# Moving the SBUF addresses of the operands of TensorE in an encoder trunk with experts

## The chip, the cores and the metric

One core of one Trainium2 chip. The metric is the device time of one execution in microseconds (us), less is better. Before the change it is 2148.49 us, the median of three runs (2148.49 to 2149.2).

## What is computed

A trunk of two layers over 256 tokens of width 1024, in float32. Each layer takes a root-mean-square norm, projects it to 59 tiles of columns for four token mixers (dilated attention, a conformer convolution, a state-space scan, a Fourier mix), gates and adds their outputs, and projects them back. Then comes a feed-forward part: dense SwiGLU (2816 wide) in layer 0, and in layer 1 a mixture of 8 experts, each SwiGLU 3584 wide, of which each token takes two. A gated per-layer embedding closes each layer.

```python
for l in range(DEPTH):
    xn = rmsnorm(h, norm_mix[l])
    u = xn @ w_in[l]
    branches = (attention_branch(...), conformer_branch(...), ssd_branch(...), fourier_branch(...))
    for i, br in enumerate(branches):
        mixed = mixed + jax.nn.sigmoid(xn @ w_gate[l, i] + b_gate[l, i]) * br
    h = h + mixed @ w_out[l]
    xn = rmsnorm(h, norm_ffn[l])
    h = h + (swiglu(xn, w1, w3, w2) if l % 2 == 0 else moe_swiglu(xn, router, w1, w3, w2))
    h = h + jax.nn.sigmoid(h @ ple_gate[l]) * (p[l] @ ple_proj[l])
return rmsnorm(h, final_norm)
```

## The kernel before

**Split products.** Almost every product is taken in three pieces. An operand is split into a high part in the format fp32r and a low part, the rest after the high part is taken away. `three` (L895) then issues three matmuls into the same sum: high by high (L897), high by low (L898 or L899) and low by high (the other). Each has its own stationary operand of 128 columns, which TensorE loads with an LDWEIGHTS, and a moving operand of 256 columns (tokens) or 512 (in the experts). The profile names a matmul `ps<-moving,stationary`.

**Weights.** SyncE loads them in blocks of 1 MB into a ring of six (`ring`). ScalarE copies one half block (a unit, 128x1024) to a high buffer (`whi` at L1563 for dense and experts; `gate_high_a`, `_b`, `_c` at L1331, `query_key_high` and `query_key_high_x` at L1317 and `out_high` at L1342 in the mixers). VectorE subtracts it from the ring and writes the low part (`wlo` at L2128, in most of the mixers `ring_lo`, L1750, L1905, L1916, L1925). Semaphores hand each unit on: ring loaded, high, low, used.

**Which operand stands still.** In the mixers, the dense part and the embedding, the weights are stationary and the tokens (`xhi`, `xlo`; `hhi`, `hlo` for the hidden layer) move, 256 columns each. The one exception are the token-major projections, where the tokens are stationary and the weights move (256 matmuls on each of L897 to L899). In the experts each pass gathers up to 128 tokens of one expert into columns 0 to 127 of `xhi` and `xlo` (L1614, L2254). These are stationary and the weights move, 512 columns at a time (`up_unit`, L1092 on). The hidden layer is transposed back (L1121), split into `hhi` and `hlo` (L1642, L2277), and is stationary for the second product (`step`). Eight passes of 14 chunks run.

**The order** of all this is written out by hand for each engine and held by semaphores alone.

**Addresses.** `sb` and `msb` take buffers from SBUF one behind the other, each size rounded up to 32 bytes. A buffer opened and left at once (`with nc.sbuf_tensor(...)`: `pass`) gives its place to the next ones, so that `ring` and `ring_lo`, or `xn` and `out_high`, lie over each other. Sizes of `pk`, `cst`, `passes_sb` and `ast` are rounded up with `LINE` so that nearly all buffers begin on a 64-byte boundary. All slices that TensorE takes step in multiples of 512 bytes, or begin 4 bytes in, so that a buffer's first address gives its place within 256 bytes.

Of the kernel before, what the change touches and what calls it, by code (L numbers as in the profile page):

```python
# [29 lines left out]
P = 128  # L30
# [110 lines left out]
BK = TT * SEQ + 2 * P  # L141
LINE = 16
DUALS = HP * TT
# [3 lines left out]
def trunk_program(nc, x, wm, wd, we, wp, pk_in, cst_in, onehot, relb, out):  # L147

    ctx = ExitStack()
    with ctx:  # L150
# [7 lines left out]


        with nc.sbuf_tensor("ring", [P, RING, BLK], F32) as ring:  # L160
            pass
# [4 lines left out]
        with nc.sbuf_tensor("out_high", [P, 2, UNIT], F32R) as ohi:  # L166
            pass
        xn = sb("xn", [P, KT, SEQ])
        xhi = sb("xhi", [P, KT, SEQ], F32R)
        xlo = sb("xlo", [P, KT, SEQ], F32R)  # L170
        pk = sb("params_sb", [P, -(-PK // LINE) * LINE])
        cst = sb("constants_sb", [P, -(-CK // LINE) * LINE])
        with nc.sbuf_tensor("query_key_high", [P, 4, UNIT], F32R) as qhi:
# [4 lines left out]
        with nc.sbuf_tensor("gate_high_c", [P, UNIT], F32R) as ghc:  # L178
            pass
        xbcp = sb("xbcp", [P, XT, SEQ + 2 * SPAD])  # L180
        with nc.sbuf_tensor("gate_high_b", [P, UNIT], F32R) as ghb:
            pass
        glu = sb("glu", [P, CT, SEQ + 2 * PAD])
        topi = sb("topi", [P, TT, 8], U32)
        cnt = sb("cnt", [P, 4])
        passes_sb = sb("passes", [P, LINE // 2], I32)
        rstd = sb("rstd", [P, SEQ])
# [25 lines left out]
        yst = msb("yst", [P, 8])  # L213
        ast = msb("ast", [P, 2, LINE])
        with nc.sbuf_tensor("mix_high", [P, KT, SEQ], F32R) as mhi:
# [32 lines left out]
        whi = sb("whi", [P, SLOTS, UNIT], F32R)  # L248
        wlo = sb("wlo", [P, SLOTS, UNIT], F32R)
        mlo = sb("mix_low", [P, KT, SEQ], F32R)  # L250
        hhi = sb("hhi", [P, 2, 2, SEQ], F32R)
# [13 lines left out]
        msk = sb("msk", [P, TT, N_EXPERTS])  # L265
        pos = sb("pos", [P, TT, MAX_PASSES + 1])


# [213 lines left out]
        def _(sp):  # L482
            sp.dma_start(h[:, :, :], x).then_inc(s_x, 16)
            load_block(sp, 0, wm[0, 0])
            sp.dma_start(cst[:, 0:CK], cst_in).then_inc(s_cst, 16)
            load_block(sp, 1, wm[0, 1])
            sp.dma_start(pk[:, 0:PK], pk_in[0]).then_inc(s_pk, 16)
            sp.dma_start(onehot_sb, onehot).then_inc(s_relL, 16)
# [68 lines left out]
        def _(pe):  # L557
# [506 lines left out]
            def experts(passes):  # L1064
# [14 lines left out]
                def up_unit(cc, u, slot, units):  # L1079

                    pe.wait_ge(s_wl, units + (u + 1))
                    for k in (2 * u, 2 * u + 1):
                        col = (k % 2) * 512
                        m = three(bank(cc % 2), both(xhi, xlo, slice(None), k, slice(0, P)),
                                  both(whi, wlo, slice(None), (slot + u) % SLOTS, slice(col, col + 512)),
                                  k == 0, k == KT - 1)
                    m.then_inc(s_wu, 1)
# [18 lines left out]
                with pe.Fori(0, n_p) as q:  # L1106
# [3 lines left out]
                    def step(k, cc, between=None):  # L1110
# [23 lines left out]
                        for half in range(2):  # L1134
                            pe.wait_ge(s_wl, units + (5 + half))
                            for col in range(0, D_MODEL, 512):
                                m = three(bank(4 + col // 512), both(hhi, hlo, slice(None), cc % 2, half, slice(0, P)),
                                          both(whi, wlo, slice(None), 2 + half, slice(col, col + 512)),
                                          cc == 0 and half == 0, cc == EXP_CHUNKS - 1 and half == 1)
# [82 lines left out]
        def _(act):  # L1222
# [383 lines left out]
            def experts():  # L1606
# [3 lines left out]
                def tokens(n):  # L1610

                    for j in range(2):
                        act.wait_ge(s_xg, n * 2 + (j + 1))
                        act.activation(xhi[:, 4 * j:4 * j + 4, 0:P], bank(6 + j).rearrange("p (c t) -> p c t", c=4),  # L1614
                                       ACT.Copy).then_inc(s_xgc, 1)
# [11 lines left out]
                with act.Fori(0, n_p) as q:  # L1627
# [4 lines left out]
                    def chunk(k, cc, j, rr):  # L1632
# [9 lines left out]
                        act.activation(hhi[:, cc % 2, :, 0:P], bank(2 + cc % 2, 0, SEQ).rearrange(  # L1642
                            "p (h t) -> p h t", h=2), ACT.Copy).then_inc(s_hh, 1)
# [62 lines left out]
            for l in range(DEPTH):  # L1706
# [13 lines left out]
                if l < DEPTH - 1:  # L1720
                    act.dma_start(pk[:, 0:PK], pk_in[DEPTH - 1]).then_inc(s_pk, 16)
            norm_root(2 * DEPTH)
# [3 lines left out]
        def _(dve):  # L1726
# [448 lines left out]
            def route():  # L2175
# [42 lines left out]
                link(dve.tensor_scalar(cnt[:, 1:2], cnt[:, 1:2], float(N_EXPERTS), None, ALU.add))  # L2218
                dve.tensor_copy(passes_sb[:, 0:1], cnt[:, 1:2]).then_inc(s_rr, 1)

# [25 lines left out]
            def experts():  # L2246
# [3 lines left out]
                def tokens(n):  # L2250

                    for j in range(2):
                        dve.wait_ge(s_xgc, n * 2 + (j + 1))
                        dve.tensor_tensor(xlo[:, 4 * j:4 * j + 4, 0:P], bank(6 + j).rearrange("p (c t) -> p c t", c=4),  # L2254
                                          xhi[:, 4 * j:4 * j + 4, 0:P], ALU.subtract).then_inc(s_xl, 1)

# [11 lines left out]
                with dve.Fori(0, n_p) as q:  # L2268
# [3 lines left out]
                    def chunk(k, cc, j):  # L2272
# [3 lines left out]
                        dve.wait_ge(s_hh, c0 + k + 1)  # L2276
                        dve.tensor_tensor(hlo[:, cc % 2, :, 0:P], bank(2 + cc % 2, 0, SEQ).rearrange(  # L2277
                            "p (h t) -> p h t", h=2), hhi[:, cc % 2, :, 0:P], ALU.subtract).then_inc(s_hl, 1)
                        if cc == EXP_CHUNKS - 2:
# [284 lines left out]
```

## Time and profile before

| | |
|---|---|
| median of three runs | 2148.49 us |
| the profiled execution, its own time | 2148.84 us |
| its span on the core | 2146.8 us |
| TensorE matmul busy | 2116.5 us (99%), 13622 matmuls |
| TensorE weight load busy | 1905.2 us (89%) |
| VectorE busy | 1684.4 us (78%) |
| ScalarE busy | 1323.6 us (62%) |
| read from HBM | 530.74 MB, 248 GB/s over the span |

The span is the time from the first to the last instruction that the profiler saw on the core; 2.0 us of the execution lie around it. A matmul's busy time in the profile is longer than the step from its start to the next one's, since matmuls overlap in the array. So TensorE's pace is read from the starts in the timeline, and not from the mean duration.

### The profile page before, as it was taken

To read this page: it belongs to the slowest core of one execution; us is meant where nothing else is said; L and a number is where in the kernel's file an instruction comes from. 1 tells how busy PE (TensorE), PEld (TensorE's weight loads), DVE (VectorE), ACT (ScalarE), POOL (GpSimd) and SP (SyncE) were. 2 spreads that over 40 slices of the span, in tenths; PEclk is the share of its full clock that TensorE was granted. 3 is DMA by queue.
4 is the path that set the end of the run, shared out by engine and by line. 5 is a ranking of instruction groups with operands and counts; after the bars stand their busy time and mean duration, and the time that the engine had idled before them with its cause. 6 is when DMAs were issued, how large, how long until landed. Compare 5 with 4: busy or idle time off the path is not lost.

```text
span 2146.8 us, 37284 instructions
## 1 busy us (share of the span) xinstructions
PE 2116.5 (99%) x13622; PEld 1905.2 (89%) x13622; DVE 1684.4 (78%) x2373; ACT 1323.6 (62%) x1864; POOL 24.3 (1%) x45
## 2 busy tenths in 40 slices
PE   9999999999999999999999999999999999999997
PEld 8999999999999999999888888888888888888886
DVE  4998866655456898766688888998989899898985
ACT  5545654454435446654467777777777777777773
POOL 0000100000000000100000000000000000000000
PEclk9999999999999999999999999999999999999998
DMA  7534436355345434435379898898999989899981
GB/s 253 188 118 154 143 142 236 138 196 176 137 158 182 164 113 169 147 132 223 138 282 364 341 350 347 345 374 328 358 350 349 347 345 369 339 361 341 351 310 76
DMA packets 74965, 533.19 MB, mean 248 GB/s; under 512 B 8655, under 2 KB 8655, under 8 KB 11000
## 3 DMA queue, kind: packets, MB, share of 16 engines
q1 hardware_dynamic: 72620, 525.04, 64.6%
q0 software_dynamic: 2048, 6.29, 1.6%
q8 instruction: 68, 1.11, 0.2%
q10 hardware_dynamic: 204, 0.54, 0.1%
q14 instruction: 25, 0.20, 0.0%
HBM read 530.74 MB, written 1.10 MB: 248 GB/s over the span
## 4 chain that ended last, share of the span: by engine, by line
PE 95%; DVE 3%; ACT 1%; DMA 1%; issue 0%; SPq 0%; DVEq 0%; ACTq 0%
PE ps L897 28%; PE ps L899 28%; PE ps L898 28%; PE ps L560 4%; PE ps L1092 1%; PE ps L1121 1%; PE ps L851 1%; PE ps L879 1%; PE ps L763 1%; PE ps L866 1%; DMA constants_sb<-constants 0%; DVE rstd L1736 0%; DVE wlo L2128 0%; PE ps L572 0%; DVE xn L1742 0%; DMA ring<-w_ple 0%
## 5 line engine op out<-in xcount | busy, mean ns | idle before, releaser
L2128 DVE TENSOR_TENSOR wlo<-ring,whi 128x1024 fp32r<-128x1024 f32 x746 | 872.8, 1220 | 145.6 <-ACT whi L1563 143.9
L1563 ACT ACTIVATE whi<-ring 128x1024 fp32r<-128x1024 f32 x746 | 749.1, 1054 | 137.9 <-PE ps L899 131.7
L897 PE MATMUL ps<-whi,xhi 128*128 128x512 f32 (+1 forms) x1160 | 434.7, 375 | 1.5 <-DVE xlo L2254 1.5
L899 PE MATMUL ps<-whi,xlo 128*128 128x512 f32 (+1 forms) x1160 | 426.8, 368 | 0.0
L898 PE MATMUL ps<-wlo,xhi 128*128 128x512 f32 x904 | 352.9, 390 | 0.0
L897 PE MATMUL ps<-xhi,whi 128*128 128x256 f32 x960 | 276.6, 288 | 2.5 <-DVE gt L2150 1.4
L898 PE MATMUL ps<-xlo,whi 128*128 128x256 f32 x960 | 273.4, 285 | 0.0
L899 PE MATMUL ps<-xhi,ring_lo 128*128 128x256 f32 x896 | 254.2, 284 | 0.0
L899 PEld LDWEIGHTS ps<-whi,xlo 128*128 128x128 f32 x1160 | 219.2, 189 | 35.8
L897 PEld LDWEIGHTS ps<-whi,xhi 128*128 128x128 f32 x1160 | 219.6, 189 | 33.6 <-DVE xlo L2254 1.9
L899 PE MATMUL ps<-xhi,wlo 128*128 128x256 f32 x704 | 199.2, 283 | 0.0
L898 PEld LDWEIGHTS ps<-wlo,xhi 128*128 128x128 f32 x904 | 170.2, 188 | 32.1
L897 PEld LDWEIGHTS ps<-xhi,whi 128*128 128x128 f32 x960 | 186.1, 194 | 4.7 <-DVE gt L2150 1.6
L898 PEld LDWEIGHTS ps<-xlo,whi 128*128 128x128 f32 x960 | 186.0, 194 | 0.3
L897 PE MATMUL ps<-whi,hhi 128*128 128x512 f32 x448 | 182.7, 408 | 0.0
L899 PE MATMUL ps<-whi,hlo 128*128 128x512 f32 x448 | 175.0, 391 | 0.0
L898 PE MATMUL ps<-wlo,hhi 128*128 128x512 f32 x448 | 174.5, 390 | 0.0
L899 PEld LDWEIGHTS ps<-xhi,ring_lo 128*128 128x128 f32 x896 | 172.4, 192 | 0.0
L1642 ACT ACTIVATE hhi<-ps 128x256 fp32r<-128x256 f32 x112 | 43.0, 384 | 187.9 <-PE ps L1121 187.9
L899 PEld LDWEIGHTS ps<-xhi,wlo 128*128 128x128 f32 x704 | 135.0, 192 | 0.0
L1750 DVE TENSOR_TENSOR ring_lo<-ring,whi 128x1024 fp32r<-128x1024 f32 x68 | 79.8, 1220 | 41.1 <-ACT whi L1242 30.2
L1453 ACT ACTIVATE gs<-ps,half_b_gate 128x256 f32<-128x256 f32 x64 | 30.2, 472 | 122.6 <-PE ps L899 122.6
(307 smaller groups left out, 3832.5 us busy)
## 6 DMA issues: line engine op xcount, KB each, us to landing
ring<-w_experts SPq DMA_DIRECT2D x340, 1024.0 KB, 5.4
ring<-w_mixers SPq DMA_DIRECT2D x114, 1024.0 KB, 4.9
ring<-w_dense SPq DMA_DIRECT2D x33, 1024.0 KB, 4.8
ring<-w_ple SPq DMA_DIRECT2D x10, 1024.0 KB, 4.9
bias<-bias_rows POOLq DMA_DIRECT2D x8, 256.0 KB, 7.1
cvfa<-bias_rows POOLq DMA_DIRECT2D x8, 256.0 KB, 5.2
constants_sb<-constants SPq DMA_DIRECT2D x1, 1048.0 KB, 9.1
h<-x_in SPq DMA_DIRECT2D x1, 1024.0 KB, 4.8
```

The source lines that it names most:

```text
L560: m = pe.matmul(dst, a, b, start=k == 0, stop=k == len(lhs) - 1)
L763: m = pe.matmul(bank(g, part * P, P), dta[:, tt, at:at + 1].to_broadcast([P, P]), con("from" if d else "upto"), start=True, stop=True)
L851: m = pe.matmul(bank(4 + u, at, n), qk[64 * u:64 * u + 64, g, i, tt * P:tt * P + P], qk[64 * u:64 * u + 64, ATT_GROUPS + g, i, key:key + n ...
L866: m = pe.transpose(bank(u, b * P, P), sa[:, u, b * P:b * P + P], con("ident"))
L897: pe.matmul(dst, lhs[0], rhs[0], start=first, stop=False, skip_group_check=True)
L898: pe.matmul(dst, lhs[0], rhs[1], start=False, stop=False, skip_group_check=True)
L899: return pe.matmul(dst, lhs[1], rhs[0], start=False, stop=last, skip_group_check=True)
L1453: act.activation(gs[:, m_ % 2, :], bank(first_bank + m_ % banks, SEQ, SEQ), ACT.Tanh, bias=half_b[:, bass.ds(b * KT + m_, 1)], scale=0.5). ...
L1563: act.activation(whi[:, slot, :], ring[:, j % RING, lo:lo + UNIT], ACT.Copy).then_inc(s_wh, 1)
L1642: act.activation(hhi[:, cc % 2, :, 0:P], bank(2 + cc % 2, 0, SEQ).rearrange("p (h t) -> p h t", h=2), ACT.Copy).then_inc(s_hh, 1)
L1750: dve.tensor_tensor(ring_lo[:, j % RING, cols], ring[:, j % RING, cols], whi[:, (2 * j + u) % SLOTS, :], ALU.subtract).then_inc(s_ed, 1)
L2128: dve.tensor_tensor(wlo[:, slot, :], ring[:, j % RING, lo:lo + UNIT], whi[:, slot, :], ALU.subtract).then_inc(s_wl, 1)
```

## The change

Five fillers of 32 bytes (`half_line_a` to `_e`, 8 float32 each) and one of 224 bytes (`home_line`) are put between the buffers, and the rounding with `LINE` goes. With the sizes added up, the operands of TensorE begin at these places within 256 bytes:

| buffer | role | before | after |
|---|---|---|---|
| `ring_lo` | stationary, mixers | 128 | 160 |
| `whi`, `wlo` | stationary; moving in the experts | 128 | 224 |
| `gate_high_a`, `gate_high_b`, `gate_high_c` | stationary | 128, 160, 64 | 224, 224, 96 |
| `query_key_high`, `query_key_high_x`, `out_high` | stationary | 64, 128, 128 | 96, 160, 160 |
| `xhi`, `xlo` | moving; stationary in token-major projections | 128 | 192 |
| `hhi`, `hlo`, `mix_low` | moving | 128 | 0 |
| `mix_high`, `branch_high`, `ybr_low` | moving | 128 | 128 |
| the experts' tokens | stationary | 128 (`xhi`, `xlo`) | 224 (`expert_high`, `expert_low`) |
| the experts' hidden layer | stationary | 128 (`hhi`, `hlo`) | 224 (`expert_hidden_high`, `_low`) |

The ring moves from 128 to 160 with `ring_lo`. No instruction is added, taken away or moved on any engine, and no wait is changed: each writes or reads at another address. In the experts the gathered tokens and the split hidden layer get four buffers of their own in place of the front columns of `xhi`, `xlo`, `hhi` and `hlo`.

```diff
-LINE = 16
+HALF_LINE = 8
+HOME_LINE = 56
...
+        sb("half_line_a", [P, HALF_LINE])
         with nc.sbuf_tensor("ring", [P, RING, BLK], F32) as ring:
             pass
         ring_lo = sb("ring_lo", [P, RING, BLK], F32R)
...
         xn = sb("xn", [P, KT, SEQ])
+        sb("half_line_b", [P, HALF_LINE])
         xhi = sb("xhi", [P, KT, SEQ], F32R)
         xlo = sb("xlo", [P, KT, SEQ], F32R)
-        pk = sb("params_sb", [P, -(-PK // LINE) * LINE])
-        cst = sb("constants_sb", [P, -(-CK // LINE) * LINE])
+        pk = sb("params_sb", [P, PK])
+        cst = sb("constants_sb", [P, CK])
...
+        sb("half_line_c", [P, HALF_LINE])
         with nc.sbuf_tensor("gate_high_b", [P, UNIT], F32R) as ghb:
             pass
         glu = sb("glu", [P, CT, SEQ + 2 * PAD])
+        sb("half_line_d", [P, HALF_LINE])
...
         wlo = sb("wlo", [P, SLOTS, UNIT], F32R)
+        sb("half_line_e", [P, HALF_LINE])
         mlo = sb("mix_low", [P, KT, SEQ], F32R)
...
+        sb("home_line", [P, HOME_LINE])
+        ehi = sb("expert_high", [P, KT, P], F32R)
+        elo = sb("expert_low", [P, KT, P], F32R)
+        ghi = sb("expert_hidden_high", [P, 2, 2, P], F32R)
+        glo = sb("expert_hidden_low", [P, 2, 2, P], F32R)
...
-                        m = three(bank(cc % 2), both(xhi, xlo, slice(None), k, slice(0, P)),
+                        m = three(bank(cc % 2), both(ehi, elo, slice(None), k),
...
-                                m = three(bank(4 + col // 512), both(hhi, hlo, slice(None), cc % 2, half, slice(0, P)),
+                                m = three(bank(4 + col // 512), both(ghi, glo, slice(None), cc % 2, half),
```

The writers of these buffers on ScalarE (L1614, L1642) and VectorE (L2254, L2277) change in the same way.

## Rows read from the trace of the kernel before

**Rows 1.** The page: span, and busy time of each engine.
```profile
span 2146.8 us, 37284 instructions
PE 2116.5 (99%) x13622; PEld 1905.2 (89%) x13622; DVE 1684.4 (78%) x2373; ACT 1323.6 (62%) x1864; POOL 24.3 (1%) x45
```
**Rows 2.** The page: the chain that ended last, by engine and by line.
```profile
PE 95%; DVE 3%; ACT 1%; DMA 1%; issue 0%; SPq 0%; DVEq 0%; ACTq 0%
PE ps L897 28%; PE ps L899 28%; PE ps L898 28%; PE ps L560 4%; PE ps L1092 1%; PE ps L1121 1%; PE ps L851 1%; PE ps L879 1%; PE ps L763 1%; PE ps L866 1%; DMA constants_sb<-constants 0%; DVE rstd L1736 0%; DVE wlo L2128 0%; PE ps L572 0%; DVE xn L1742 0%; DMA ring<-w_ple 0%
```
**Rows 3.** Stages (mixers of layer 0, dense, experts): from:to, us, busy, clock, DMA share.
```profile
100.00:400.00 300.00, 298.16 (x2510) 289.42 (x2509) 234.01 (x438) 160.71 (x285) 8.66 (x12) 1.00 0.42 147
400.00:580.00 180.00, 175.91 (x1439) 174.91 (x1438) 94.44 (x100) 79.75 (x96) 0.31 (x4) 0.99 0.53 192
1092.00:2080.00 988.00, 988.00 (x4571) 815.53 (x4570) 882.95 (x995) 743.19 (x921) 0.00 (x0) 1.00 0.92 350
```
**Rows 4.** Matmuls of L897 alone in three stretches; L898 and L899 issue as many.
```profile
0.00:1070.00 1070.00, 674.11 (x2352) 0.99 0.46 166
1070.00:2085.00 1015.00, 540.68 (x1341) 1.00 0.90 345
```
**Rows 5.** Groups of instructions by shape: forms that stand apart, matmuls.
```profile
L897 PE MATMUL ps<-whi,xhi 128*128 128x512 f32 x904 | 362.3, 401 | 1.5 <-DVE xlo L2254 1.5
L897 PE MATMUL ps<-whi,hhi 128*128 128x512 f32 x448 | 182.7, 408 | 0.0
L898 PE MATMUL ps<-ring_lo,xhi 128*128 128x256 f32 x256 | 72.4, 283 | 0.0
L897 PE MATMUL ps<-xhi,query_key_high 128*128 128x256 f32 x256 | 72.9, 285 | 0.0
L897 PE MATMUL ps<-xhi,gate_high_c 128*128 128x256 f32 x64 | 17.8, 278 | 0.0
```
**Rows 6.** Timeline, dense-type steps at one common offset: start, us, matmul.
```profile
600.07 0.28 PE L897 MATMUL ps<-xhi,whi 128*128 128x256 f32 x1
...
601.51 0.28 PE L897 MATMUL ps<-xhi,whi 128*128 128x256 f32 x1
```
**Rows 7.** Timeline, a gate in layer 0: units in `gate_high_a`, then in `gate_high_b`.
```profile
237.34 0.28 PE L897 MATMUL ps<-xhi,gate_high_a 128*128 128x256 f32 x1
...
238.66 0.28 PE L899 MATMUL ps<-xhi,ring_lo 128*128 128x256 f32 x1
238.78 0.28 PE L897 MATMUL ps<-xhi,gate_high_b 128*128 128x256 f32 x1
...
240.08 0.28 PE L899 MATMUL ps<-xhi,ring_lo 128*128 128x256 f32 x1
```
**Rows 8.** Timeline, a query and key block in layer 0.
```profile
143.02 0.28 PE L897 MATMUL ps<-xhi,query_key_high 128*128 128x256 f32 x1
...
144.44 0.28 PE L897 MATMUL ps<-xhi,query_key_high 128*128 128x256 f32 x1
...
144.78 0.28 PE L897 MATMUL ps<-xhi,query_key_high 128*128 128x256 f32 x1
...
147.26 0.28 PE L897 MATMUL ps<-xhi,query_key_high 128*128 128x256 f32 x1
```
**Rows 9.** Timeline, experts: a steady stretch.
```profile
1501.17 0.39 PE L897 MATMUL ps<-whi,xhi 128*128 128x512 f32 x1
...
1503.21 0.39 PE L897 MATMUL ps<-whi,xhi 128*128 128x512 f32 x1
```
**Rows 10.** Timeline, experts: a stretch behind a transpose.
```profile
1108.65 0.39 PE L898 MATMUL ps<-wlo,xhi 128*128 128x512 f32 x1
...
1109.81 0.39 PE L897 MATMUL ps<-whi,xhi 128*128 128x512 f32 x1
```
**Rows 11.** ScalarE's splits: `gate_high_a`, then `gate_high_b`; ns min/median/max.
```profile
L1331 ACT ACTIVATE gate_high_a<-ring x16: 1042/1049/1053, 218.1 to 941.3; 128x1024 fp32r<-128x1024 f32 x16
L1331 ACT ACTIVATE gate_high_b<-ring x8: 1048/1053/1057, 219.0 to 929.7; 128x1024 fp32r<-128x1024 f32 x8
```

More of the change, by code:

```diff
@@ L183, in trunk_program @@
         glu = sb("glu", [P, CT, SEQ + 2 * PAD])
+        sb("half_line_d", [P, HALF_LINE])
         topi = sb("topi", [P, TT, 8], U32)
         cnt = sb("cnt", [P, 4])
-        passes_sb = sb("passes", [P, LINE // 2], I32)
+        passes_sb = sb("passes", [P, 1], I32)
         rstd = sb("rstd", [P, SEQ])
@@ L213, in trunk_program @@
         yst = msb("yst", [P, 8])
-        ast = msb("ast", [P, 2, LINE])
+        ast = msb("ast", [P, 2, 4])
         with nc.sbuf_tensor("mix_high", [P, KT, SEQ], F32R) as mhi:
@@ L484, in _ @@
             load_block(sp, 0, wm[0, 0])
-            sp.dma_start(cst[:, 0:CK], cst_in).then_inc(s_cst, 16)
+            sp.dma_start(cst[:, :], cst_in).then_inc(s_cst, 16)
             load_block(sp, 1, wm[0, 1])
-            sp.dma_start(pk[:, 0:PK], pk_in[0]).then_inc(s_pk, 16)
+            sp.dma_start(pk[:, :], pk_in[0]).then_inc(s_pk, 16)
             sp.dma_start(onehot_sb, onehot).then_inc(s_relL, 16)
@@ L1613, in tokens @@
                         act.wait_ge(s_xg, n * 2 + (j + 1))
-                        act.activation(xhi[:, 4 * j:4 * j + 4, 0:P], bank(6 + j).rearrange("p (c t) -> p c t", c=4),
+                        act.activation(ehi[:, 4 * j:4 * j + 4, :], bank(6 + j).rearrange("p (c t) -> p c t", c=4),
                                        ACT.Copy).then_inc(s_xgc, 1)
@@ L1641, in chunk @@
                         act.wait_ge(s_ht, c0 + k + (1 - DENSE_CHUNKS))
-                        act.activation(hhi[:, cc % 2, :, 0:P], bank(2 + cc % 2, 0, SEQ).rearrange(
+                        act.activation(ghi[:, cc % 2, :, :], bank(2 + cc % 2, 0, SEQ).rearrange(
                             "p (h t) -> p h t", h=2), ACT.Copy).then_inc(s_hh, 1)
@@ L1720, in _ @@
                 if l < DEPTH - 1:
-                    act.dma_start(pk[:, 0:PK], pk_in[DEPTH - 1]).then_inc(s_pk, 16)
+                    act.dma_start(pk[:, :], pk_in[DEPTH - 1]).then_inc(s_pk, 16)
             norm_root(2 * DEPTH)
@@ L2218, in route @@
                 link(dve.tensor_scalar(cnt[:, 1:2], cnt[:, 1:2], float(N_EXPERTS), None, ALU.add))
-                dve.tensor_copy(passes_sb[:, 0:1], cnt[:, 1:2]).then_inc(s_rr, 1)
+                dve.tensor_copy(passes_sb[:, :], cnt[:, 1:2]).then_inc(s_rr, 1)
                 dve.wait_ge(s_re, 1)
@@ L2253, in tokens @@
                         dve.wait_ge(s_xgc, n * 2 + (j + 1))
-                        dve.tensor_tensor(xlo[:, 4 * j:4 * j + 4, 0:P], bank(6 + j).rearrange("p (c t) -> p c t", c=4),
-                                          xhi[:, 4 * j:4 * j + 4, 0:P], ALU.subtract).then_inc(s_xl, 1)
+                        dve.tensor_tensor(elo[:, 4 * j:4 * j + 4, :], bank(6 + j).rearrange("p (c t) -> p c t", c=4),
+                                          ehi[:, 4 * j:4 * j + 4, :], ALU.subtract).then_inc(s_xl, 1)
                 def add(n, m_):
@@ L2276, in chunk @@
                         dve.wait_ge(s_hh, c0 + k + 1)
-                        dve.tensor_tensor(hlo[:, cc % 2, :, 0:P], bank(2 + cc % 2, 0, SEQ).rearrange(
-                            "p (h t) -> p h t", h=2), hhi[:, cc % 2, :, 0:P], ALU.subtract).then_inc(s_hl, 1)
+                        dve.tensor_tensor(glo[:, cc % 2, :, :], bank(2 + cc % 2, 0, SEQ).rearrange(
+                            "p (h t) -> p h t", h=2), ghi[:, cc % 2, :, :], ALU.subtract).then_inc(s_hl, 1)
                         if cc == EXP_CHUNKS - 2:
```

## The prediction

> **What bounds the kernel now.** I read the page first. TensorE is busy for 2116.5 of 2146.8 us [rows 1], and 95% of the chain that ended last is TensorE's, 84% of it on the three lines of the split product, L897, L898 and L899 [rows 2]. Next came the stages: in the mixers TensorE is busy 298.16 of 300 us, in the dense part 175.91 of 180, in the experts 988.00 of 988 [rows 3]. VectorE, the next engine, stands at 234.01 of 300 (78%) and at 882.95 of 988 (89%), the transfers at a share of 0.42 and 0.92, and the granted clock is 1.00, that is 2.4 GHz. So nothing but the pace of the matmuls sets the time, and what a matmul saves or loses in its step to the next one arrives at the end nearly whole.
>
> The pace is what one must see here, and it is in the starts. In dense-type work twelve steps take 601.51 - 600.07 = 1.44 us, 120.0 ns each for 256 columns [rows 6]. In the experts nine steps take 1503.21 - 1501.17 = 2.04 us, 226.7 ns each for 512 columns [rows 9]. The difference of 256 columns costs 106.7 ns, which is 2.4 GHz at one column a cycle. Taken from the 120.0 it leaves 13.3 ns that each matmul pays whatever its length. The weight load of the next matmul runs beside each of these, so the 13.3 ns may hold a quarrel between the moving stream and the weight load over the SBUF, and that quarrel may hang on addresses.
>
> **What addresses do in the trace of before.** It has a small experiment built in. The stationary buffers of almost all matmuls begin at 128 within 256 bytes and so do the moving ones, but `gate_high_b` is at 160 (32 bytes past a 64-byte boundary, just what the change wants everywhere) and `query_key_high` and `gate_high_c` are at 64. Same line, same shape, same stage:
> - `gate_high_a` with `ring_lo`, all at 128: eleven steps in 238.66 - 237.34 = 1.32 us, 120.0 ns [rows 7].
> - `gate_high_b` with `ring_lo`: eleven steps in 240.08 - 238.78 = 1.30 us, 118.2 ns [rows 7]. The starts are rounded to 10 ns, so this is known to 0.9 ns either way.
> - `query_key_high` with `ring_lo`: 36 steps in 147.26 - 143.02 = 4.24 us, 117.8 ns [rows 8], known to 0.3 ns.
>
> In both of the faster stretches only two of three weight loads come from the shifted buffer; the third is of `ring_lo` and still at 128. So shifting helps, by about 2 ns of 120, and the steps become uneven: three of them take 144.78 - 144.44 = 0.34 us, 113 ns each [rows 8].
>
> The Trainium skill speaks against any gain: "TensorE: Matmul & The Clock Gate", section "Step-by-step: what each phase is for", says that TensorE has two independent read ports to SBUF, one for the moving operand and one for LDWEIGHTS, and that loading the next weights takes nothing from the running matmul. By that rule the time would stay at 2148.8 us; rows 7 and 8 disagree with it by 1.8 to 2.2 ns a step. The same page's "Wait — 56ns, not 53.3ns?" gives N / 2.4 GHz + 2.5 ns from start to start, an estimate of 109.2 ns for 256 columns, which rows 6 miss by 10.8 ns; by that figure there would be that much to win.
>
> **The change part by part.** Engines, order and waits are the same, so the sum is a count of matmuls times a price.
>
> *Count.* The three lines issue 3 x 2352 = 7056 matmuls before 1070 us [rows 4], all of 256 columns, and 64 each in the last embedding; with 192 on the first blocks' own lines (L600, L606, L984 to L992) that is 7440. In the experts they issue 3 x (904 + 448) = 4056 of 512 columns [rows 5]. Of the 7440, 3 x 256 = 768 are token-major, with tokens stationary [rows 5]; 2 x 256 + 2 x 64 = 640 have a stationary buffer at 64 already [rows 5], 128 have `gate_high_b`. This leaves 5904 that go from a common offset to a stationary buffer 32 past and a moving one on the boundary.
>
> *Price.* The rows give 118.2 (two of three loads at 32) and 117.8 (two of three at 64) against 120.0. With all three shifted the saving could stay as it is, or grow by half: 120 - 1.5 x 2.2 = 116.7 ns. I take 117.5, a saving of 2.5 ns, between these. The ends are 1.8 and 3.3 ns. 5904 x 2.5 ns = 14.8 us (10.6 to 19.5).
>
> *Token-major projections.* Here the weights move at 32 past and the tokens stand on the boundary. The distance between the two is the same, the other way round; no row shows this order. I price it as the others: 768 x 2.5 ns = 1.9 us, between 0 and 2.5.
>
> *Already shifted.* 640 matmuls at 117.8 go to 117.5, 0.2 us; the 128 of `gate_high_b` gain as little.
>
> *Experts.* Both streams move from 128 to 224, together. Their distance stays zero. If only the distance counts, the 226.7 ns stay: 0. It is the term I know least, since no row has both streams at one common offset that is not on a 64-byte boundary. Bounds: the same experts' code runs at (1109.81 - 1108.65) / 5 = 232 ns behind a transpose [rows 10], 5.3 ns more at the same addresses, only in another phase; as much gained, by the difference that 256-column rows show between the evenest and the shifted steps (2.2 ns), is 4056 x 2.2 = 9 us. From 21.5 us lost to 9 us gained, then. I take 0, because both the distance and the steady pace it goes with are unchanged.
>
> *The other engines.* The splits of ScalarE write `whi` at 32 past now. `gate_high_b` is such a buffer: 1053 ns against 1049 for `gate_high_a` [rows 11], nothing. In the experts VectorE has 11% and the mixers 22% of slack over TensorE to cover it [rows 3]; were that cover gone, each percent on VectorE would show. The own buffers of the experts take no wait away, since the order was held by the same semaphores.
>
> *Sum.* 14.8 + 1.9 + 0.2 = 16.9 us, all on TensorE's path. From the profiled execution's 2148.84 us (its median is 2148.49, 0.35 less) this makes 2131.9, with 2126 to 2138 from the price's ends. Nothing else is close enough to give it back: a TensorE 2% faster in the mixers stays well over VectorE's 78%. The clock stays at 2.4 GHz, since no idle time is added.
>
> **The rivals.**
> 1. *Shifted streams settle in the good phase.* Rows 8 show steps of 113 ns among the others. If with all buffers shifted every step locks there, 6672 x 6.7 ns = 45 us go: 2104. For it: steady stretches do lock (120.0 over and over in rows 6). Against: rows 7 and 8 never stay there. Were all of the fixed 13.3 ns to go, as far as the 2.5 ns, it would be more; I hold that for unlikely.
> 2. *The experts pay for leaving the boundary* (slower). The moving weights there now begin 32 past, and a row of 2048 bytes then reaches over one more 64-byte piece. If this puts the 4056 long matmuls at the 232 ns of rows 10, they lose 21.5 us, and the sum is +4.6: 2153.4. It decides from 16.9 us / 4056 = 4.2 ns a matmul; partly lost (2 ns) it leaves 2140. For it: the experts are half of the time and do show 232 in some phases. Against: distance unchanged.
> 3. *Nothing changes.* What made rows 7 and 8 faster could be the mixture of offsets and not the distance, and with a uniform shift the even 120.0 comes back: 2148.8.
> 4. *The transfers slow down.* The ring begins 32 bytes past a boundary too. In the experts the queues are busy for a share of 0.92 [rows 3]; from packets 1 / 0.92 = 8.7% longer on, TensorE would wait for weights, and each further percent costs 9.9 us. No row bears on it.
>
> **How the numbers follow.** Forecast 0.42, rival 1 0.18, rival 2 0.22 (of it 0.15 slower, 0.04 within 0.2%, 0.03 still faster), rival 3 0.14, rival 4 0.04. A measurement of this kernel tells 0.2% (4.3 us) from no change. Faster: 0.42 + 0.18 + 0.03 + 0.03 (of rival 3, which may hide a small gain) = 0.66. Slower: 0.15 + 0.04 + 0.01 (of rival 3) = 0.20. Same, from what is left of rivals 2 and 3: 0.14. The likeliest case gives 2132. The range runs from rival 1's 2104 to 2156, just past rival 2's 2153; left out are a gain over 2% and the transfers.
>
> **What would show it.** In the changed profile, steps of about 117.5 ns in the dense part, so that twelve take 1.41 us where they took 1.44; 226.7 ns in the steady experts; DVE and ACT rows within 10 ns of these. Steps of 120.0 in the dense part prove the main term wrong; steps over 231 ns in the steady experts prove rival 2; matmuls of the experts waiting for `wlo` or the ring would show rival 4.

## The result, and the profile after

The changed kernel takes 2139.01 us (median of ten runs, 2138.39 to 2143.43) against 2148.12 for the kernel before in the same series: a ratio of 0.9963, 95% interval 0.9953 to 0.9972. The medians lie 9.1 us apart, and the ratio stands for 7.9 us with an interval from 6.0 to 10.1: faster, by about half of the 16.9 us that were forecast. The sign was right and the place was right; the size was not.

The page of the changed kernel (answers to [rows 1] and [rows 2]; all lines from `three` on stand 11 further down, so that L897 to L899 are now L908 to L910):

```profile
span 2136.7 us, 37284 instructions
PE 2106.8 (99%) x13622; PEld 1893.7 (89%) x13622; DVE 1684.7 (79%) x2373; ACT 1324.8 (62%) x1864; POOL 24.3 (1%) x45
...
PE 95%; DVE 3%; ACT 1%; DMA 1%; issue 0%; SPq 0%; DVEq 0%; ACTq 0%
```

The instructions are the same in number and the chain is still TensorE's. VectorE and ScalarE are as busy as before to within 1.2 us, although nearly every buffer that they write has moved. TensorE's busy time fell by 9.7 us and the span by 10.1 us.

Where in the program it fell is read from three landmarks that both kernels have: the first products of the dense part (L984, now L995), the seeding of the experts' sums (L1101, now L1112) and the last scatter behind the experts (L1160, now L1171). The lines are from the views of one line each, of before and then of after; the two numbers behind the durations are the first and the last start, us.

```profile
L984 PE MATMUL ps<-xhi,whi x32: 278/283/581, 424.2 to 438.8; 128*128 128x256 f32 x32
...
L1101 PE MATMUL ps<-sca,constants_sb x8: 379/379/382, 1078.4 to 1079.9; 128*128 128x256 f32 x8
...
L1160 PE MATMUL ps<-sca,yx x16: 379/379/483, 2094.2 to 2097.5; 128*128 128x256 f32 x16
```

```profile
L995 PE MATMUL ps<-xhi,whi x32: 277/281/388, 421.7 to 434.7; 128*128 128x256 f32 x32
...
L1112 PE MATMUL ps<-sca,constants_sb x8: 379/379/382, 1068.0 to 1069.5; 128*128 128x256 f32 x8
...
L1171 PE MATMUL ps<-sca,yx x16: 379/379/483, 2084.2 to 2087.5; 128*128 128x256 f32 x16
```

The mixers of layer 0 gained 2.5 us, everything from there to the experts another 7.9, and the experts lost 0.4, which is less than the 2.4 us between the fastest and the slowest of ten runs of the kernel before. The mixers of layer 0 hold 2688 products of the three lines (counted in the trace between the landmarks) and gained 0.9 ns on each; the stretch behind them holds 4368 and gained 1.8. So the gain is not even over matmuls of one shape.

The timeline of the changed kernel shows why. A dense chunk (12 steps, answers to [rows 6]), a query and key block (36 steps, answers to [rows 8]) and a steady stretch of the experts (8 steps, answers to [rows 9]):

```profile
542.00 0.28 PE L909 MATMUL ps<-xlo,whi 128*128 128x256 f32 x1
...
543.41 0.28 PE L909 MATMUL ps<-xlo,whi 128*128 128x256 f32 x1
```

```profile
142.00 0.28 PE L908 MATMUL ps<-xhi,query_key_high 128*128 128x256 f32 x1
...
146.32 0.28 PE L908 MATMUL ps<-xhi,query_key_high 128*128 128x256 f32 x1
```

```profile
1491.01 0.39 PE L908 MATMUL ps<-whi,expert_high 128*128 128x512 f32 x1
...
1492.82 0.39 PE L910 MATMUL ps<-whi,expert_low 128*128 128x512 f32 x1
```

The dense chunk takes 1.41 us for twelve steps, 117.5 ns, the number that was forecast (starts rounded to 10 ns make it good to 0.8 ns; over all steps of this kind the saving is 2.2 ns, as the table below shows). The query block takes 4.32 us for 36 steps, 120.0 ns, where it took 4.24 before, 117.8 [rows 8]: it has become slower. The experts take 1.81 us for eight, 226.3 ns, with starts rounded to 10 ns the same as before.

Both traces hold the same 13622 matmuls in the same order, so that each step of one can be set beside the same step of the other. Summed by where the moving operand and the next stationary one stand within 256 bytes, before and after (distance = stationary minus moving):

```text
256 columns             distance before   distance after     count   difference us   ns each
xhi, xlo with whi, wlo, gates 0             32                2991     -6.66          -2.2
hhi, mix_low with whi         0             224 (32 behind)   1051     -3.04          -2.9
xhi, xlo with ring_lo         0             224               1188     -1.43          -1.2
other kinds                   0             32 to 160          614     -0.62          -1.0
query_key_high, gate_high_c   192           160                630     +1.27          +2.0
token-major                   0             224 or 32          764     -0.55          -0.7
512 columns (experts)         0             0                 3895     +1.96          +0.5
```

(In the third row stand the steps to `query_key_high_x` too; in the other kinds those from `mix_high`, `branch_high` and `ybr_low`, and from `hhi` to `out_high`.) The cost seems to follow the distance, and `query_key_high`, which had a good distance before, seems to have been moved to a poor one; the sweep below tests both.

### The profile page after: what moved, and what is told of

Same layout as the page of the kernel before. It is cut to its first block, busy times and chain, and to the rows that moved or that the text cites. A ratio compares the mean times of both kernels' runs of the same rounds, so it can differ in the third digit from the quotient of the medians.

```text
span 2136.7 us, 37284 instructions
## 1 busy us (share of the span) xinstructions
PE 2106.8 (99%) x13622; PEld 1893.7 (89%) x13622; DVE 1684.7 (79%) x2373; ACT 1324.8 (62%) x1864; POOL 24.3 (1%) x45
## 4 chain that ended last, share of the span: by engine, by line
PE 95%; DVE 3%; ACT 1%; DMA 1%; issue 0%; SPq 0%; DVEq 0%; ACTq 0%
PE ps L908 28%; PE ps L910 28%; PE ps L909 28%; PE ps L571 4%; PE ps L1103 1%; PE ps L1132 1%; PE ps L862 1%; PE ps L890 1%; PE ps L774 1%; PE ps L877 1%; DMA constants_sb<-constants 0%; DVE rstd L1747 0%; DVE wlo L2139 0%; PE ps L583 0%; DMA ring<-w_ple 0%; DVE xn L1753 0%
## 5 line engine op out<-in xcount | busy, mean ns | idle before, releaser
L908 PE MATMUL ps<-whi,expert_high 128*128 128x512 f32 x904 | 363.4, 402 | 0.5 <-DVE expert_low L2265 0.5
L910 PE MATMUL ps<-whi,expert_low 128*128 128x512 f32 x904 | 354.5, 392 | 0.0
L909 PE MATMUL ps<-wlo,expert_high 128*128 128x512 f32 x904 | 353.2, 391 | 0.0
L908 PE MATMUL ps<-xhi,whi 128*128 128x256 f32 x960 | 273.9, 285 | 2.6 <-DVE gt L2161 1.4
L910 PE MATMUL ps<-xhi,ring_lo 128*128 128x256 f32 x896 | 253.0, 282 | 0.0
L910 PEld LDWEIGHTS ps<-whi,expert_low 128*128 128x128 f32 x904 | 169.6, 188 | 37.0
L908 PEld LDWEIGHTS ps<-whi,expert_high 128*128 128x128 f32 x904 | 169.9, 188 | 33.1 <-DVE expert_low L2265 0.9
L909 PEld LDWEIGHTS ps<-wlo,expert_high 128*128 128x128 f32 x904 | 170.2, 188 | 32.7
L910 PE MATMUL ps<-xhi,wlo 128*128 128x256 f32 x704 | 197.6, 281 | 0.0
L908 PEld LDWEIGHTS ps<-xhi,whi 128*128 128x128 f32 x960 | 182.3, 190 | 4.7 <-DVE gt L2161 1.6
L908 PE MATMUL ps<-whi,expert_hidden_high 128*128 128x512 f32 x448 | 181.9, 406 | 0.0
L910 PE MATMUL ps<-whi,expert_hidden_low 128*128 128x512 f32 x448 | 175.2, 391 | 0.0
L909 PE MATMUL ps<-wlo,expert_hidden_high 128*128 128x512 f32 x448 | 175.0, 391 | 0.0
L910 PEld LDWEIGHTS ps<-xhi,ring_lo 128*128 128x128 f32 x896 | 170.0, 190 | 0.0
L1653 ACT ACTIVATE expert_hidden_high<-ps 128x256 fp32r<-128x256 f32 x112 | 42.9, 383 | 187.2 <-PE ps L1132 187.2
L910 PEld LDWEIGHTS ps<-xhi,wlo 128*128 128x128 f32 x704 | 132.7, 188 | 0.0
```

What stands on the lines that cost most here:

```text
L908: pe.matmul(dst, lhs[0], rhs[0], start=first, stop=False, skip_group_check=True)
L909: pe.matmul(dst, lhs[0], rhs[1], start=False, stop=False, skip_group_check=True)
L910: return pe.matmul(dst, lhs[1], rhs[0], start=False, stop=last, skip_group_check=True)
L1653: act.activation(ghi[:, cc % 2, :, :], bank(2 + cc % 2, 0, SEQ).rearrange("p (h t) -> p h t", h=2), ACT.Copy).then_inc(s_hh, 1)
```

## The experiments

Three theories stood: **D**, only the distance between the two streams counts; **A**, the stationary operand's place within 64 bytes counts; **C**, traffic of the other engines or the transfers makes the cost, and addresses only shift it.

### A sweep over places

Behind TensorE's last work on the kernel before, steady runs of matmuls are added. Nothing of the trunk's own work is touched. VectorE ends and the output is written during the first three runs (32, 64 and 96 stationary columns, up to 2147.4 us); beside the runs behind them VectorE, ScalarE and the transfers are idle.

```diff
+            def sweep(cols, times, place, width=P):
+                pe.matmul(bank(6, 0, SEQ), gs[:, 0, 0:P], gs[:, 0, :], start=True, stop=True)
+                for i in range(times):
+                    at = i % 2 * 512 + place[0]
+                    by = i % 4 * P + place[1]
+                    if cols == 512:
+                        at = place[0]
+                    pe.matmul(bank(i % 6, 0, cols)[0:width], wlo[:, i % 3, by:by + width], whi[:, i % 4, at:at + cols],
+                              start=True, stop=True, skip_group_check=True)
...
+            for moving in range(0, 64, 8):
+                for still in range(0, 64, 8):
+                    sweep(256, 24, (moving, still))
...
```

> The kernel before, with some 2500 more matmuls put at its end, when all other engines are done: steady runs of fp32r matmuls with the stationary operand from wlo and the moving one from whi, each at 0, 32, ... 224 bytes past the buffers' 128, every pair of places, 24 matmuls of 256 columns and 12 of 512 for each pair; also 32, 64, 96 and 128 stationary columns, and places 4 to 112 bytes apart that are no multiple of 32. Theory D (the distance between the two streams sets the cost): all pairs at distance 0 give 120.0 ns for 256 columns and 226.7 for 512, pairs at other distances 116 to 118.5 and 223 to 225, whatever the moving stream's own place. Theory A (the place of the stationary operand within 64 bytes sets it): 117.5 in every second row, 120.0 in the others, at any distance. Theory C (traffic of ScalarE, VectorE or the transfers sets it): here, with these idle, all pairs alike, near 110. If the 13.3 ns belong to the weight load's reads, 64 stationary columns cost half of them (about 113 to 114 ns), 32 a quarter.

The mean step of each run behind its first ones, ns, worked out from the starts in the trace (row: place of the moving operand, column: of the stationary one, bytes past 128; five of eight rows for 256 columns, three for 512):

```text
256    0     32     64     96    128    160    192    224
  0  119.7  118.4  113.3  118.6  118.7  119.8  117.8  116.5
 32  117.7  119.7  118.4  117.8  117.4  118.5  120.1  117.8
 64  117.7  116.8  119.7  118.3  113.6  118.5  120.1  119.7
 96  120.0  117.7  116.8  119.7  118.3  113.3  117.3  120.1
128  118.9  119.8  117.8  116.8  120.0  118.3  117.8  118.7
512    0     32     64     96    128    160    192    224
  0  228.4  232.7  233.7  234.3  232.4  233.7  228.4  233.3
 32  233.4  226.6  233.6  233.0  234.3  234.0  233.0  228.9
 64  229.3  233.3  230.3  233.4  233.0  234.3  233.9  233.1
```

The table for 256 columns runs along its diagonals: 119.7 to 120.0 at distance 0, 119.7 to 120.1 at 160 and 117.7 to 117.8 at 192 whatever the row, and in seven of the eight rows 118.2 to 118.4 at 32 and 116.5 to 116.8 at 224. The 2 ns between 192 and 160 are the 2.0 ns that `query_key_high` and `gate_high_c` lost. At 96 and 128 the rows differ, by up to 1.5 and 1.9 ns, so the distance does not settle everything. Theory A, which wants columns, falls, and so does C: with all other engines idle, distance 0 costs the same 120.0 as in the kernel. Two things nobody had expected. Distance 64 shows either 113.3 to 113.6 or 117.8. And for 512 columns distance 0 is among the best two of its row (226.6 to 230.3), with distance 192 at 228.4 to 229.3; the others cost mostly 232 to 234. These runs have only 12 matmuls, and in six of eight rows 192 is lower than 0; the longer runs further down decide between them.

How much belongs to the weight load is seen when fewer stationary columns are loaded. The timeline of the same kernel, runs of 24 with 32, 64, 96 and 128 stationary columns at distance 0; the second number is the run's time, us:

```profile
2137.94 3.09 PE L1226 MATMUL ps<-whi,wlo 128*32 128x256 f32 x24
2141.11 3.09 PE L1226 MATMUL ps<-whi,wlo 128*64 128x256 f32 x24
2144.28 3.14 PE L1226 MATMUL ps<-whi,wlo 128*96 128x256 f32 x24
2147.50 3.23 PE L1226 MATMUL ps<-whi,wlo 128*128 128x256 f32 x24
```

From 128 to 64 columns the run gets 0.14 us shorter, and from 64 to 32 nothing. The steps are 120.0, 113.6 and 113.5 ns. So of the 13.3 ns over 106.7, some 6.7 vanish with 64 stationary columns (and with a good distance), and 6.7 do not. Fewer stationary columns also mean that fewer partitions of the sum are written, so this alone does not show that the weight load is what costs.

### The whole layout moved together

```diff
+        sb("half_line_a", [P, 8])
         with nc.sbuf_tensor("ring", [P, RING, BLK], F32) as ring:
```

> The kernel before with one filler of 32 bytes ahead of the ring and nothing else: nearly all buffers move together by 32 bytes, stationary and moving ones alike. Theory D: distances are as before, steps of 120.0 and 226.7, total 2148 (within 2 us). Theory A: the stationary ones stand 32 bytes past a 64-byte boundary, the mixers and the dense part gain as in the changed kernel, total about 2139. Rival of the prediction (a stream off the 64-byte boundary costs): over 2155.

2148.6 us against 2148.59, ratio 1.0001 (0.9991 to 1.001). Nearly every stationary operand now stands 32 bytes past a 64-byte boundary, as in the changed kernel, and nothing is won; nearly every stream is off the boundary, and nothing is lost: the 3895 steps between the experts' long matmuls agree on average with those of before within 0.1 ns. Theory A and rival 2 of the prediction fall together.

### The experts' own buffers

First the changed kernel with the experts back in the shared buffers:

```diff
-                        m = three(bank(cc % 2), both(ehi, elo, slice(None), k),
+                        m = three(bank(cc % 2), both(xhi, xlo, slice(None), k, slice(0, P)),
...
-                                m = three(bank(4 + col // 512), both(ghi, glo, slice(None), cc % 2, half),
+                                m = three(bank(4 + col // 512), both(hhi, hlo, slice(None), cc % 2, half, slice(0, P)),
```

> The changed kernel, but the experts read and write the front columns of xhi, xlo, hhi and hlo as before, so that their stationary operands stand at 192 and 0 and the moving weights at 224. Theory D, with the saving carried over from 256 columns: each of the 4056 long matmuls falls from 226.7 to about 224.5, the experts gain 9 us, total about 2130. Rival (long streams want distance 0, which is what the own buffers are for): 229 to 232 ns, total 2148 to 2160. If the own buffers are worth nothing: 2139.

2157.46 us, ratio 1.0046 (1.0029 to 1.0063): slower than the kernel before, and 18 us over the changed one. Nine steps of its experts, from the timeline:

```profile
1360.16 0.39 PE L910 MATMUL ps<-whi,xlo 128*128 128x512 f32 x1
...
1362.26 0.39 PE L910 MATMUL ps<-whi,xlo 128*128 128x512 f32 x1
```

2.10 us for nine, 233.3 ns and not 226.7. Over the whole trace 2591 such steps between long matmuls now stand at distance 224 and took 5.1 ns more than in the kernel before, and 1304 at distance 32 took 3.8 ns more, 18.2 us together. The sweep's 233 for distance 224 is confirmed inside the kernel, and the saving carried over from 256 columns, which Theory D's number here rested on, has the wrong sign for long streams.

Then the own buffers alone, in the kernel before, at the place that everything else has:

```diff
+        sb("fill_d", [P, 64])
+        ehi = sb("expert_high", [P, KT, P], F32R)
+        elo = sb("expert_low", [P, KT, P], F32R)
+        ghi = sb("expert_hidden_high", [P, 2, 2, P], F32R)
+        glo = sb("expert_hidden_low", [P, 2, 2, P], F32R)
```

> The kernel before with the experts' four own buffers at 128 within 256 bytes, where xhi and whi are too, and nothing else moved. Distance 0 as before, so steps of 226.7 as before and 2148 within 2 us by theory D: own buffers win nothing by themselves, they only keep the distance at 0 when the others move. If their closer packing (512 bytes from one slice to the next and not 1024) is worth something: 2140 or less.

2147.33 us, ratio 0.9998 (0.9989 to 1.0008): nothing. The own buffers win no time; they keep the experts from losing 18 us when the others move.

### Other distances

A finer sweep looked for the best distance.

> As the first sweep, the matmuls at the end of the kernel before: moving operand at 128, stationary operand 0, 4, 8 ... 252 bytes further, every 4 bytes, 24 matmuls of 256 columns and 12 of 512 each; 512 columns with 32, 64, 96 and 128 stationary columns; and distance 64 again from each of the eight places of the moving operand, twice. From the first sweep: 120 at 0, 115.5 at 8, 113.3 or 117.8 at 64, 116.5 at 224, nowhere below 113.3. For 512 columns 226.6 or 230 at 0, and with 32 or 64 stationary columns 220 (213.3 and the same 6.8 ns that 113.5 has over 106.7). If the cost of distance 64 hangs on the place, the same four places (0, 64, 96, 192 past the buffer's start) give 113.3 again; if it hangs on the phase in which a run begins, others do.

Steps at distances 0, 4, 8 ... 28 bytes: 120.0, 118.3, 115.5, 116.9, 118.2, 119.9, 118.7, 116.7 ns. The lowest value, 113.3 to 113.6, comes at 52, 64, 76, 88 and 168, and none is below. At 64 each of the eight moving places was tried twice: 113.3 to 113.6 nine times, 117.8 seven times; five places gave one of each. For 512 columns nothing beat the 226.6 that distance 0 showed in the first sweep; 16 and 120 bytes came to 226.6 and 226.7, in runs of 12 matmuls. The first is taken up again below, the second was not. The expected 220 for fewer stationary columns did not come: 224 to 236 ns, uneven, with 32 or 64 columns too. The means of 32, 64, 96 and 128 stationary columns lie between 229.6 and 230.4. So what long streams pay does not shrink with the weight load, and what it is stays open.

The kernel was then laid out anew with one distance throughout. Tokens come first, a filler behind them sets the distance, and small buffers serve as the other fillers:

```diff
+        xhi = sb("xhi", [P, KT, SEQ], F32R)
+        xlo = sb("xlo", [P, KT, SEQ], F32R)
+        sb("fill_a", [P, 16])
         with nc.sbuf_tensor("ring", [P, RING, BLK], F32) as ring:
...
+        topi = sb("topi", [P, TT, 8], U32)
+        cnt = sb("cnt", [P, 4])
         with nc.sbuf_tensor("query_key_high", [P, 4, UNIT], F32R) as qhi:
...
+        half_b = sb("half_b_gate", [P, N_BRANCHES * KT])
+        passes_sb = sb("passes", [P, LINE // 2], I32)
         with nc.sbuf_tensor("gate_high_b", [P, UNIT], F32R) as ghb:
...
+        sb("fill_c", [P, 48])
         mlo = sb("mix_low", [P, KT, SEQ], F32R)
```

> The kernel with the operands placed anew: every moving buffer of the mixers, the dense part and the embedding at 128 within 256 bytes, every stationary one at 192, so 64 bytes further; the experts' own buffers at 192 like the weights that move there (distance 0). Theory D with the sweep's better value: steps of 113.3 ns in the dense part, about 6600 matmuls by 6.7 ns, 44 us less than before, about 2105. With the sweep's other value (117.8): 6600 by 2.2, 14.5 less, 2134. If only the 32-byte offset of the change does it (theory A): 2148.

2115.85 us, ratio 0.9846 (0.9829 to 0.9862), 31 us under the kernel before and 23 under the changed one. Twelve steps of its dense part:

```profile
530.55 0.28 PE L907 MATMUL ps<-xlo,whi 128*128 128x256 f32 x1
...
531.91 0.28 PE L907 MATMUL ps<-xlo,whi 128*128 128x256 f32 x1
```

1.36 us, 113.3 ns. Of 5844 steps that went from distance 0 to 64, 3847 took 113 or 114 ns and 1581 took 117 or 118: both patterns, which is why the result lies between the two expected numbers, nearer to the better.

The same layout at 32 and at 224, by other fillers (`fill_a` is shown; those that bring the later moving buffers and the experts' tokens back to their places follow it):

```diff
-        sb("fill_a", [P, 16])
+        sb("fill_a", [P, 8])
```

> As the run at distance 64, but every stationary buffer of 256-column matmuls 32 bytes past its moving one (160 against 128), in the mixers as in the dense part; experts at distance 0. The sweep's 118.4 and the changed kernel's 117.8 for this distance make 1.6 to 2.2 ns for 6600 matmuls, 11 to 15 us: 2133 to 2137, some 3 us below the changed kernel, since query_key_high is no longer at another distance.

```diff
-        sb("fill_a", [P, 16])
+        sb("fill_a", [P, 56])
```

> The same with every stationary buffer 224 bytes past (32 bytes behind) its moving one: 96 against 128. The sweep gave 116.5 to 116.8 at seven of eight places, and the changed kernel 117.0 where hhi at 0 meets whi at 224: 3.0 to 3.4 ns for 6600, 20 to 22 us, 2126 to 2128. By theory A nothing tells this from the run before it, as both stationary buffers are 32 bytes past a 64-byte boundary.

At 32: 2137.15 us, ratio 0.9956 (0.9939 to 0.9972). At 224: 2127.71 us, ratio 0.9909 (0.9892 to 0.9925). Twelve dense steps at 224:

```profile
539.01 0.28 PE L907 MATMUL ps<-xlo,whi 128*128 128x256 f32 x1
...
540.41 0.28 PE L907 MATMUL ps<-xlo,whi 128*128 128x256 f32 x1
```

1.40 us, 116.7 ns. The two kernels have the same stationary place within 64 bytes and differ by 9.4 us, in the order of the sweep and by about its amount (1.7 ns on some 6600 steps would be 11 us). The second came out within the range named ahead of the run, the first 0.2 us above its end. The token-major steps do not follow the sweep: at distance 224 (in the layout at 32) they gained 1.0 ns each, and at distance 32 (in the layout at 224) 0.8, where the sweep has 3.3 and 1.7. Why is open.

### Two patterns at one distance, and a miss

> Steady runs at the end of the kernel before again, 256 columns, at the distances of 8, 32, 52, 64, 76, 88, 168, 224 and 0 bytes, each eight times with a matmul of another length ahead of it. So far 64 gave 113.3 in about half of the runs and 117.8 in the others. If the start of a run picks one of two steady patterns at this distance alone, one of 52, 76, 88 and 168 gives 113.3 every time; if every distance but 0 has several patterns, all of them vary and only 0 stays at 120.0.

At 52, 76 and 168 all eight runs took 113.3 to 113.4 ns, once the first eight steps were past. At 64 and 88 seven of eight did, and the first took 117.8 and 116.7. At 8, 32, 224 and 0 all took the same within 0.3 ns (115.5, 118.3, 116.7, 120.0). Rows of the timeline, first series, at distance 52 and then 64; second series (another matmul ahead), at 52, 64, 224 and 0:

```profile
2146.04 3.77 PE L1226 MATMUL ps<-whi,wlo 128*128 128x256 f32 x30
2149.89 3.89 PE L1226 MATMUL ps<-whi,wlo 128*128 128x256 f32 x30
...
2181.82 3.89 PE L1226 MATMUL ps<-whi,wlo 128*128 128x256 f32 x31
...
2185.90 3.89 PE L1226 MATMUL ps<-whi,wlo 128*128 128x256 f32 x31
...
2202.22 3.97 PE L1226 MATMUL ps<-whi,wlo 128*128 128x256 f32 x31
...
2206.38 4.07 PE L1226 MATMUL ps<-whi,wlo 128*128 128x256 f32 x31
```

In the first series 64 costs 0.12 us more than 52 over 30 matmuls; in the second they are equal. So at 64 the start of a run picks one of two steady patterns.

Distance 52 promised to be the safe choice. In the kernel it was made by beginning the moving buffers 12 bytes later:

```diff
+        def tokens_buffer(flat, lo, n):
+            return flat[:, lo + 3:lo + 3 + n * SEQ].rearrange("p (k t) -> p k t", k=n)
+
+        x_both = sb("tokens_split", [P, 2 * KT * SEQ + 8], F32R)
+        xhi = tokens_buffer(x_both, 0, KT)
+        xlo = tokens_buffer(x_both, KT * SEQ, KT)
```

> The run at distance 64 with its moving buffers xhi, xlo, hhi, hlo and mix_low begun 12 bytes later, so that the stationary ones stand 52 bytes past them; the three buffers of the mixers' branches stay at 64. Distance 64 fell into 117.8 in part of its stretches, 52 gave 113.3 in all eight phases. About 6000 matmuls at 113.3 and not at 120.0 are 40 us, 44 with the rest at 64: 2104 to 2108, against 2115.9 at distance 64. If the streams of the real kernel, which change between buffers, fall out of the good pattern as often as at 64: 2116. If a start that is no multiple of 16 or 32 bytes costs by itself: over 2120.

It did not: 2136.77 us, ratio 0.9941 (0.9928 to 0.9955), 12 us won where 40 to 44 were expected. Its dense steps:

```profile
543.81 0.28 PE L912 MATMUL ps<-tokens_split,whi 128*128 128x256 f32 x1
...
545.22 0.28 PE L912 MATMUL ps<-tokens_split,whi 128*128 128x256 f32 x1
```

1.41 us for twelve, 117.5 ns. In the sweeps the stationary operand had carried the 52 bytes and the moving one had stood on a 32-byte multiple. One more sweep took the two apart.

> Steady runs of 256 columns at the end of the kernel before: the moving operand 0, 4, 8, 12, 16, 24 or 32 bytes past the buffer's start and the stationary one 0, 32, 52, 64 or 224 bytes further than it, three phases each. The run at distance 52 in the kernel won only a third of what 52 promised in the sweep. If it is the moving operand's start off a 32-byte multiple that costs, distance 52 gives 113.3 from 0 and 32 and 116 to 118 from 12, and distance 64 too is worse from 4, 8 and 12 than from 0. If distance 52 gives 113.3 from every start, the sweep's streams are too simple, and the kernel's own order of buffers is what keeps it from the good pattern.

Steps at distance 52: 113.3 with the moving operand at 0, and 117.7 to 117.8 with it at 12, in all three phases. Timeline, second series: moving at 0, distances 0, 32, 52; then moving at 12, distances 0, 32, 52.

```profile
2277.72 4.07 PE L1226 MATMUL ps<-whi,wlo 128*128 128x256 f32 x31
...
2281.98 4.02 PE L1226 MATMUL ps<-whi,wlo 128*128 128x256 f32 x31
...
2286.19 3.90 PE L1226 MATMUL ps<-whi,wlo 128*128 128x256 f32 x31
...
2341.26 4.06 PE L1226 MATMUL ps<-whi,wlo 128*128 128x256 f32 x31
...
2345.51 4.00 PE L1226 MATMUL ps<-whi,wlo 128*128 128x256 f32 x31
...
2349.70 4.00 PE L1226 MATMUL ps<-whi,wlo 128*128 128x256 f32 x31
```

The run of the last row has steps of 117.8 ns, which agrees with the kernel's 117.5. At 12, distance 64 took 116.7, a little less than 52. With the moving operand at 4, 8 or 24, distances 52 and 64 both cost 120; at 16 distance 64 keeps 113.3; at 32 distance 64 does in two phases of three, and 52 costs 120.0. So "only the distance counts" holds at most for moving operands on multiples of 32 bytes and distances that are such multiples too (and there not at 96 and 128), and not below that. A kernel with the stationary operands moved by 52 and the moving ones left at 128 was not tried.

### Long streams

> Steady runs of 512 columns at the end of the kernel before, at the distances of 0, 16, 52, 64, 104, 168, 192 and 224 bytes, each eight times with a matmul of another length ahead. In the kernels distance 0 gives 226.7 most of the time and 231 to 236 in stretches. If each distance but 0 costs more in every phase, 0 gives 226.7 in most runs and the others 229 to 234: this is why the experts' tokens must stay at the weights' place. If 16 or 104 gives 226.6 every time, or less, the experts can win from another distance too.

Distance 0 took 226.6 to 228.2 ns over eight phases behind the first four steps, and 226.6 to 226.7 in every phase behind the first ten. 192 took 228.6 to 229.1, and 16, 52, 64, 104, 168 and 224 all took 233.1 to 233.6 in every phase. So the 226.6 that distance 16 had shown before was the short run's. In one series, distances 0, 64 and 192:

```profile
2223.55 5.35 PE L1226 MATMUL ps<-whi,wlo 128*128 128x512 f32 x22
...
2240.43 5.47 PE L1226 MATMUL ps<-whi,wlo 128*128 128x512 f32 x22
...
2257.45 5.40 PE L1226 MATMUL ps<-whi,wlo 128*128 128x512 f32 x22
```

For streams of 512 columns the old distance 0 is the best of those that were tried in these longer runs, which is what the experts' own buffers keep.

## Why the prediction was off

**What bounds the kernel**: right. TensorE's pace set the time in all the kernels with other places, and what its steps won or lost came through to the end.

**The price of 2.5 ns for 5904 matmuls (14.8 us)**: this is the step that failed most, a term that was mis-sized by 3.0 us. It measured 11.8 us, 2.0 ns each on 5844 steps. The direction came rightly from `gate_high_b` [rows 7] and `query_key_high` [rows 8], but I took a stretch at distance 32 and one at distance 192 for two readings of one effect, "shifted", and went beyond both of them. They are two different distances with different costs, and the changed kernel holds a mixture: 2.2 ns at 32, 2.9 at 224 from one moving place, 1.2 at 224 in mixed streams. Growing the saving by half because one load of three was unshifted was an argument and not a reading. Distance 32 itself, read from rows 7 alone, gave 1.8 ns and 10.6 us, the low end that stood in the text and the better forecast. That the cost follows the relative place is shown; why it does is not. The "quarrel" of two reads in the SBUF that the prediction supposes was tested by no run.

**The token-major projections (1.9 us)**: 0.55 us over the 764 steps that went to 224 or 32. The first sweep shows that the sign of the distance matters (118.4 at 32, 116.5 to 116.8 at 224), so "the same the other way round" had no ground. It does not explain the small gain either, since 224 is the better of the two there.

**"Already shifted, 0.2 us"**: wrong in sign. `query_key_high` and `gate_high_c` went from distance 192 to 160 and lost 1.3 us, 2 ns each. The table of places in the change had both numbers; I looked at the place within 64 bytes and not at the difference to `xhi`.

**The experts, 0**: right within the spread of the runs (+0.4 us by the landmarks, +2.0 us on the steps between long matmuls; at the same distance 0 those steps came to +0.9 to -0.9 us in the layouts at 32, 64 and 224), and for the right reason, the distance kept. The bounds of 21.5 lost and 9 gained were far too wide, and the run with shared buffers shows what the width was about: at another distance they lose 18 us.

**The sum**: 11.8 + 0.6 - 1.3 - 2.0 is 9.1 us where 16.9 stood; the other 1.0 of the 10.1 us between the profiles lies in steps from or to other lines (in the experts such steps gained 1.5 us, which is why their landmarks show less than 2.0). 2132 was forecast and 2139 measured, within the range of 2104 to 2156 and outside the likeliest case's own 2126 to 2138.

**Rival 1** (the good pattern, 113.3) exists, but not at the distance that the change chose: it was seen at 64 and gives 2115.85. (The three steps of 113 ns that the prediction reads in rows 8 are 0.34 us between rounded starts, good to 3 ns each; unrounded they are 116.) **Rival 2** (a stream off the boundary costs) fell with the layout that was moved as a whole. **Rival 3** (nothing changes) fell with the result. The rule of the Trainium skill, "TensorE: Matmul & The Clock Gate", section "Step-by-step: what each phase is for", that loading the next weights takes nothing from the running matmul, is not borne out: with all else idle and equal instructions the sweeps have 6.7 ns a step between distances 0 and 52. The other figure of the Trainium skill, same page, section "Wait — 56ns, not 53.3ns?", which makes an estimate of 109.2 ns for 256 columns, was reached by no steady run; the lowest is 113.3. **Rival 4**: the transfers hold 1% of the chain after as before, and the experts kept their pace.

## What to carry to other kernels

Where a kernel is bound by short matmuls that each load new weights, read the step between starts in the timeline, compare it for buffers at different places, and compute for each pair the distance from moving to stationary operand within 256 bytes, since that and not an alignment rule told most of the times apart here. Sweep the distances in steady runs at the end of the kernel itself, in several phases and for each stream length, before laying out buffers; here 64 bytes was worth 1.5% for 256 columns, while in the sweep it cost the 512-column streams 6.6 ns a step. Vary in the sweep the same operand that the layout will move.

## What the runs showed of the hardware that was not expected

- Two steady patterns at one distance: 113.3 and 117.8 ns at 64 bytes. At one place, only what ran ahead differed between them.
- A floor of 113.3 to 113.6 ns for 256 columns, reached by a good distance as well as by loading 64 stationary columns in place of 128. The 6.7 ns above 106.7 that remain were not explained.
- The sign and the optimum turn with the stream's length: at 224 bytes 256 columns gain 3.3 ns a step and 512 columns lose 6.6.
- A moving operand that begins 4, 8 or 24 bytes past a 32-byte multiple had 120 ns at each of the distances 32, 52, 64 and 224 (up to 121.8), so that these shifts undid the gain.
